# Narrower products in the feed-forward layers of an eight-block float32 kernel: 512 columns become two of 256, and one or two products per piece are cut unevenly

## The reference

```
def swiglu(x, w_in, w_out):
    a, b = jnp.split(x @ w_in, 2, axis=-1)
    return (jax.nn.silu(a) * b) @ w_out

x = x + 0.5 * swiglu(rmsnorm(x, ffn1_norm[l]), w_ffn1_in[l], w_ffn1_out[l])
```

## Time and profile before

| | us |
|---|---|
| median of three runs | 2610.45 |
| the profiled execution | 2613.06 |
| its span, first to last instruction | 2611.1 |
| PE busy (MATMUL), 19726 instructions | 2570.1 |
| PEld busy (LDWEIGHTS), 19726 instructions | 2352.6 |
| POOL busy | 2032.2 |
| ACT busy | 1286.5 |
| DVE busy | 878.6 |
| mean granted TensorE clock | 0.998 |

### The profile page before, as it was taken

The page is one execution under the profiler, slowest core; times in us unless marked ns, Lnnn a source line. Parts: engine busy times, 40 slices in busy tenths (PEclk is TensorE's granted clock), DMA queues, the critical chain, the costliest instruction groups (busy, mean ns, idle before and its releaser), DMA issues.

```text
span 2611.1 us, 48248 instructions
## 1 busy us (share of the span) xinstructions
PE 2570.1 (98%) x19726; PEld 2352.6 (90%) x19726; DVE 878.6 (34%) x1518; ACT 1286.5 (49%) x1934; POOL 2032.2 (78%) x906
## 2 busy tenths in 40 slices
PE   7999999999999999999999999999999999999998
PEld 6999999899899989989989998998998989899897
DVE  2744364211243436411121133733122131474212
ACT  4445555444444555544444445754444444574443
POOL 7988666888898866688888886478888878547886
PEclk9999999999999999999999999999999999999999
DMA  6566544555656653655555566245556556535554
GB/s 236 187 202 202 192 135 135 194 187 193 207 183 198 208 186 131 172 195 190 188 196 193 178 189 215 98 170 189 190 182 202 192 171 201 187 98 179 194 192 137
DMA packets 128738, 474.79 MB, mean 182 GB/s; under 512 B 14432, under 2 KB 14432, under 8 KB 127520
## 3 DMA queue, kind: packets, MB, share of 16 engines
q1 hardware_dynamic: 124704, 454.09, 52.3%
q0 software_dynamic: 3840, 17.83, 2.4%
HBM read 469.24 MB, written 2.62 MB: 181 GB/s over the span
## 4 chain that ended last, share of the span: by engine, by line
PE 50%; DVE 4%; ACT 2%; DMA 1%; issue 0%; POOL 0%; DVEq 0%; SPq 0%; ACTq 0%
PE psA L381 29%; PE psY L381 19%; PE psT L432 1%; DMA ring<-in_weights 1%; DVE psY L1279 0%; ACT upper L1876 0%; DVE psY L1267 0%; PE psT L654 0%; ACT xT_upper L1876 0%; DVE st L1364 0%; DVE x L1294 0%; POOL rest L1065 0%; ACT G L1907 0%; DVE Sc L1339 0%; DVE Sc L1819 0%
## 5 line engine op out<-in xcount | busy, mean ns | idle before, releaser
L1065 POOL TENSOR_TENSOR rest<-ring,upper 128x1024 fp32r<-128x1024 f32 (+1 forms) x834 | 1992.5, 2408 | 513.1 <-ACT upper L1876 502.5
L1876 ACT ACTIVATE upper<-ring 128x1024 fp32r<-128x1024 f32 (+1 forms) x834 | 870.4, 1053 | 786.2 <-DMA ring<-in_weights 785.2
L381 PE MATMUL psA<-xT_upper,upper 128*128 128x256 f32 x2784 | 381.5, 280 | 0.6 <-ACT arena L1876 0.6
L381 PE MATMUL psA<-xT_upper,rest 128*128 128x256 f32 x2784 | 379.4, 279 | 0.0
L381 PE MATMUL psA<-xT_rest,upper 128*128 128x256 f32 x2784 | 378.9, 279 | 0.0
L1320 DVE TENSOR_TENSOR psA<-sil,psA 128x256 f32<-128x256 f32 x144 | 61.8, 429 | 926.4 <-ACT sil L1876 926.2
L381 PEld LDWEIGHTS psA<-xT_upper,upper 128*128 128x128 f32 x2784 | 358.7, 188 | 14.3 <-ACT arena L1876 1.3
L381 PEld LDWEIGHTS psA<-xT_upper,rest 128*128 128x128 f32 x2784 | 347.5, 189 | 0.0
L381 PEld LDWEIGHTS psA<-xT_rest,upper 128*128 128x128 f32 x2784 | 347.3, 188 | 0.0
L381 PE MATMUL psY<-upper,hT_upper 128*128 128x512 f32 x704 | 203.9, 395 | 1.3 <-DVE hT_rest L1322 1.3
L381 PE MATMUL psY<-upper,hT_rest 128*128 128x512 f32 x704 | 204.5, 396 | 0.0
(11 more groups left out here) (282 smaller groups left out, 2997.5 us busy)
## 6 DMA issues: line engine op xcount, KB each, us to landing
ring<-in_weights SPq DMA_DIRECT2D x862, 512.0 KB, 3.6
G<-in_rows POOLq DMA_DIRECT2D x6, 1024.0 KB, 6.7
G<-in_rows POOLq DMA_DIRECT2D x7, 512.0 KB, 5.7
arena<-rel_by_distance POOLq DMA_DIRECT2D x8, 256.0 KB, 7.8
x<-in_x SPq DMA_DIRECT2D x2, 512.0 KB, 5.8
par<-in_params POOLq DMA_DIRECT2D x4, 256.0 KB, 5.7
xn<-in_mem POOLq DMA_DIRECT2D x1, 1024.0 KB, 11.2
memory_transposed<-arena POOLq DMA_DIRECT2D x1, 1024.0 KB, 5.5
```

The lines of the kernel that those rows point to most:

```text
L381: i = pe.matmul(out, lhsT, rhs, start=start, stop=stop)
L1065: pool.tensor_tensor(rest[:, r, 0:n], ring[:, r, 0:n], upper[:, r, 0:n], ALU.subtract)\
L1876: act.activation(out, in_, func, **kw).then_inc(*up)
```

## The change

Three places are edited. `down` makes each 512-column product as two over the same stationary block, normally 256 and 256 columns. In a down that is followed by an up (all but `down(0)` to `down(2)`; `up_next` says so), the last product of the last round is cut as 240 and 272 instead. `up` passes `end=144` for its second piece, and `by_parts` then makes that piece's last product as 144 and 112 columns. The tail, the group's route, the projections and the mixers keep their products. Nothing changes in the order of work between pieces, in what is loaded, or on the other engines.

```diff
-            def by_parts(out, s, up, rhs=xT):
+            def by_parts(out, s, up, rhs=xT, end=S):
 
                 for a_, b_, first, last in passes():
                     for k in range(KD):
-                        mm(out, s[a_][:, k], rhs[b_][:, k], first and k == 0, last and k == KD - 1,
-                           up if last and k == KD - 1 else None)
+                        for c in (slice(0, end), slice(end, S)) if last and k == KD - 1 and end < S else (slice(0, S),):
+                            mm(out[:, c], s[a_][:, k], rhs[b_][:, k, c], first and k == 0, last and k == KD - 1 and c.stop == S,
+                               up if last and k == KD - 1 and c.stop == S else None)
@@
-                        by_parts(out[:, v * S:(v + 1) * S], s, filled(lab) if v == 1 else None)
+                        by_parts(out[:, v * S:(v + 1) * S], s, filled(lab) if v == 1 else None, end=S if v == 0 else 144)
@@
-                def down(j):
+                def down(j, up_next=True):
@@
-                                mm(ys[2 * t + n], hT[v][:, j % HIDDEN, t * P:(t + 1) * P], s[w][:, n * 512:(n + 1) * 512],
-                                   first and j == 0, False)
+                                cut_at = S - 16 if up_next and last and (t, n) == (TT - 1, 1) else S
+                                for c in (slice(0, cut_at), slice(cut_at, 512)):
+                                    mm(ys[2 * t + n][:, c], hT[v][:, j % HIDDEN, t * P:(t + 1) * P],
+                                       s[w][:, n * 512 + c.start:n * 512 + c.stop],
+                                       first and j == 0 and c.start == 0, False)
@@
-                    down(j)
+                    down(j, up_next=j == GROUP - 1)
```

## The result

| | before | after |
|---|---|---|
| median, us | 2609.43 | 2628.74 |
| lowest to highest, us | 2607.73 to 2612.09 | 2628.54 to 2632.53 |
| the profiled execution, us | 2613.06 | 2628.55 |
| its span, us | 2611.1 | 2626.7 |
| mean granted TensorE clock | 0.998 | 0.999 |

Both medians are over four runs. The ratio is 1.0077, with a 95% interval of 1.0064 to 1.009. The prediction was 2599 us with a range up to 2617, so the sign was wrong and the range missed it by 12 us. The granted clock is the same, so the clock doesn't explain the difference.

The account below looks back on a forecast made before the run. PE, busy 98% of the span, was taken to bound the kernel by its pace of streaming products. Terms of -9.0 - 2.5 - 0.6 - 1.2 + 0.9 + 0.8 = -11.6 us took 2610.45 to 2599 us, range 2581 to 2617.

Parts of the forecast that it names:

- the first sentence of the terms: Likeliest case, chance 0.42: all 256-column products stay at the quick level of 113.4 ns, -11.6 us in all.
- the 120 ups: Single ups, each 5.55 us with its cut: -6.3 us against slow ones, +5.7 against quick ones, together -0.6 us.
- The mixed rival: Ups alternate with downs quick (+4.6 us), or ups quick with downs slow (+4.4 us): both 2615 us, chance 0.20.
- the last two terms: The cut in `up(4)`, +0.9 us, and the 240 and 272 columns in downs, +0.8 us.
- the pairs: Pairs of ups, one in each of eight blocks: -1.2 us in the likeliest case, +2.1 us if all is slow.
- the slow cases: The mixed cases at 2615 us, chance 0.20, and everything on the slow level at 2643 us, chance 0.14.
- Slower begins at 26% slow: Point between all quick (-11.6 us) and all slow (+33 us), 44.6 us apart, from which the kernel was to be slower.
- the rival of the free cut: The up's two short products stream behind their own loads, 113 ns together: 2582 us, chance 0.14.
- the slow case: Everything settles on the slow level, a single up lasting 5.76 us: +33 us, 2643 us, chance 0.14.
- the quick case: Likeliest case, single downs of 24 products at 113.4 ns, 2.72 us in place of 2.795: -9.0 us over 120.
- the rival that the change doesn't bite: Down halves keep 116.5 ns and cuts cost only where ups are slow, or their loads are partly skipped: near 2610 us, chance 0.10.
- The evidence for the quick level: Argument against the all-slow rival (chance 0.14): quick is commoner after transposes, the tail and long 512-column streams.

Follow-up runs that it names:

- e1: The changed kernel without either cut, so downs as 256 and 256 columns and ups whole: 2600.62 us, ratio 0.9968 to the kernel before.
- e10: The changed kernel without its cuts, with each down's first product and its last before an up as 272 and 240: 2590.32 us, ratio 0.9937.
- e3: The changed kernel with all downs as 256 and 256, only the up's 144/112 cut kept: 2627.63 us, ratio 1.007.
- e5: The changed kernel without 240/272 and with the up's last product as 128 and 128: 2627.59 us, ratio 1.0064.
- e12: The kernel before with hT 128 bytes lower, no product cut: 2596.78 us, ratio 0.9963.
- e6: The changed kernel without its cuts, with the first product of each down as 272 and 240: 2616.09 us, ratio 1.0021.
- e9: The kernel before with hT 64 bytes lower, no product cut: 2609.72 us, ratio 1.0004.
- e15: The kernel before with hT 64 bytes lower and only the last product before an up cut, as 272 and 240: 2588.58 us, ratio 0.9923.
- e7: The changed kernel without its cuts, with hT 64 bytes lower: 2608.58 us, ratio 0.9987.

## Why the prediction was wrong

**The step that failed** is the first sentence of the terms: "with 256-column products everywhere the state stays at the quick level". It rested on the reading of the earlier trace rows that a down of 512 columns turns the state and 256-column products keep it. The second half is right: an uncut up lasts 5.46 or 5.66 us in every one of these kernels and seldom anything between, so it keeps its level to its end. The first half is not: it isn't the width that turns the level but the change between the operands of an up and those of a down, and at which level the next piece lands follows from the level before, the operands' addresses and the columns of the products at the seam. Halves alone turned it at nearly every seam (e1), and two shifts of 16 columns stopped that (e10). Nor did the terms give the cut of the up anything beyond its own 0.11 us: in the runs it costs 27 us (e3 less e1), 15.5 for itself and the rest through the levels. The prediction had the 120 ups at -0.6 us, and they came to +16.4, though part of the cut's own price went to the downs.

**The combination that came wasn't priced.** The mixed rival had "ups alternate, downs quick" and "ups quick, downs slow", and missed "ups slow, downs quick". By the prediction's own terms that is +24.6 for the ups, -9.0 - 2.5 for the downs and +1.7 for the last two terms, +2.1 for the pairs: +17, or 2627 us, against 2628.7 measured. A mechanism with two levels and two kinds of piece has four cases, and the table of them would have held the result. In place of that the slow cases got one number at each end, 2615 and 2643, and the range stopped at 2617. "Slower begins at 26% slow" is where the sum crosses zero; the prediction's own bound for slower, 5.2 us, lies at 38%.

**The sizes held.** Quick halves are 113.3 ns and slow ones 117.8. The cut costs 108 ns, as 112 ns a load step said (106 to 111), and not nothing: the rival of the free cut is excluded by e5 and by the starts above. Where the short products put it was unforeseen: 60 ns of it falls to the down, so the up lasts 5.70 us where the slow case said 5.76, and the down 2.81 where the quick case said 2.72. The 240/272 costs 9 ns in place of 6. Feeders and waits stayed out of it, as said, and the rival that the change doesn't bite fell.

**The evidence for the quick level** ("after transposes, the tail and long 512 streams the quick level is the commoner one") was none: what a seam between down and up does isn't drawn anew each time. In the changed kernel 112 of the 117 ups fell on one side, in e12 whole blocks did, and in e1, e6, e10 and e9 at least 115 of 117. A share of quick places elsewhere says nothing of a new seam.

**Two rules of the Trainium skill.** A quick half is 113.3 ns, eight in 0.90 us in the changed kernel, and the quickest whole is 226.7 ns, 2.72 us for twelve in e9: at its best each costs the same per column, though at two addresses of `hT`. At one address the levels decide: two halves take 227 or 236 ns against 233 in the kernel before, and 240 against 227 with `hT` 64 bytes lower. The Trainium skill, page "TensorE: Matmul & The Clock Gate", section "Wait — 56ns, not 53.3ns?", gives each product a fixed 2.5 ns, and an estimate from it is 4.6 us for the 1824 more; the best paces show none of it, and the levels move a pair by more than that. On the cut, the starts gave 344 ns in place of 236. The Trainium skill, same page, section "Architectural detail: the array is 16× 32×32, not 1× 128×128", lets a product begin before its load is complete. The trace agrees on the start: the down's first product starts at 64.72, and its load's record runs from 64.67 to 64.86. But in none of the kernels with a cut does that save anything.

**What stays open.** What holds the level between pieces, and through what, no row tells: PE shows no wait at either level and the loads' records keep their length, 188 and 189 ns. It isn't the clock, whose granted share is 1.00 in the quick up at 59.20 and in the slow one at 67.44 of the kernel before. Nor is it what else the chip does meanwhile: over that kernel's 61 quick and 56 slow ups GpSimd is busy 87 and 88% of the time, the DMA engines 60 and 59%, and VectorE 6 and 12% on average, with anything from 0 to 98% in single ups of either level; it is 8% in e1, where 115 are quick, and 9% in e6, where all are slow. The runs show that addresses and the columns at the seam choose it, not by which rule. That 272/240 lands quick in three kernels, 240/272 doesn't in the changed one, and 224/288 does with halves but not with wholes 64 bytes lower was found by trial, and so was the offset of 128 bytes. Only `hT` was moved; the addresses of the ring and of `xT` were not. Whether another kernel would follow the same shift wasn't tried.

## What to carry to other kernels

Where a stream of products shows two stable paces for the same shapes at the same granted clock, read the pace from the starts, piece by piece, and list every combination of levels with its price before naming one as likely; a change that touches the seam between two operands may exchange them all. Try the cheap knobs first, an operand's address by 64 or 128 bytes and 16 columns moved across the last product before a seam: here they are worth 20 us, while halves and wholes at their best (e10 and e15) can't be told apart. Don't cut a product below the time of its successor's load (128 float32 columns, 112 ns): each cut here cost 108 ns, and it can also set the level of the next 48 products.

## What the runs showed that was not expected

- The same 48 products last 5.46 or 5.66 us, and a single product ahead of them decides which: e6 (5.658 us) and e10 (5.479) differ by one product's 272/240, right before the up. The cut in the changed kernel does it from 25 products earlier.
- 512-column products have at least three paces at the same clock: 226.7 ns (e9, e15), 229 to 231 (e12) and 233 (the kernel before). Only the address of the stationary operand differs between e9, e12 and the kernel before.
- The same 64 bytes that make wholes quicker (233 to 227 ns, e9) make halves slower (118 to 120 ns, e7 against e1).
- With `hT` 128 bytes lower (e12) an up's level lasts through whole blocks, 15 ups with the downs between them, where in the kernel before the single downs turned it.
- A short product's cost isn't where the product is: in the changed kernel the next start came 178 ns after that of the product behind the cut, 60 ns more than the 118 of its own stream.
